# Depthwise convolution with 28 of its 31 taps on TensorE and three on ScalarE and GpSimd

## What is computed

```python
def odd_mixer(h, w_in, dw_w, dw_b, ln_g, ln_b, w_out):
    proj = h @ w_in                                  # 512 x 1024 by 1024 x 3072
    a, b, gate = jnp.split(proj, [CONV_WIDTH, 2 * CONV_WIDTH], axis=-1)
    glu = a * jax.nn.sigmoid(b)
    conv = lax.conv_general_dilated(                 # depthwise, 31 taps, causal
        glu, dw_w.astype(glu.dtype), window_strides=(1,), padding=[(CONV_K - 1, 0)],
        dimension_numbers=('NWC', 'WIO', 'NWC'), feature_group_count=CONV_WIDTH)
    cf = conv.astype(jnp.float32) + dw_b.astype(jnp.float32)
    mu = jnp.mean(cf, axis=-1, keepdims=True)
    var = jnp.mean(jnp.square(cf - mu), axis=-1, keepdims=True)
    cn = (cf - mu) * lax.rsqrt(var + EPS) * ln_g.astype(jnp.float32) + ln_b.astype(jnp.float32)
    y = jax.nn.silu(cn).astype(h.dtype) * jax.nn.silu(gate)
    return y @ w_out
```

## Time and profile before

| | us |
|---|---|
| median of 3 runs | 1090.32 |
| lowest and highest | 1090.15, 1090.68 |
| profiled execution | 1090.47 |
| its span in the trace | 1088.6 |

### The profile page before, as it was taken

How to read it: one execution, slowest core, us unless ns; L and a number is a source line. 1 busy time by engine, 2 the same in 40 slices (tenths; PEclk the granted TensorE clock), 3 DMA queues, 4 the chain that set the end, 5 groups by cost and what they waited for, 6 DMA issues and landing times.

```text
span 1088.6 us, 16129 instructions
## 1 busy us (share of the span) xinstructions
PE 1078.4 (99%) x5872; PEld 873.0 (80%) x5872; DVE 669.1 (61%) x969; ACT 458.9 (42%) x807; POOL 495.0 (45%) x373
## 2 busy tenths in 40 slices
PE   9999999999999999999999999999999999999997
PEld 7788877788888888888888888877778878888786
DVE  6877966327856676667631222558754668886863
ACT  6334421445653333333323333345464643244663
POOL 4444631132645444444444444533348577532541
PEclk9999999999999999999999999999999999999999
DMA  9953621331323232323232324322115222212222
GB/s 247 137 90 62 93 52 29 114 81 39 106 89 114 79 104 88 113 79 105 88 106 71 104 95 140 114 78 79 39 44 149 70 67 78 78 40 79 77 78 77
DMA packets 101721, 97.27 MB, mean 89 GB/s; under 512 B 4896, under 2 KB 95776, under 8 KB 101280
## 3 DMA queue, kind: packets, MB, share of 16 engines
q1 hardware_dynamic: 101232, 95.71, 32.3%
q10 hardware_dynamic: 432, 0.79, 0.2%
HBM read 94.38 MB, written 2.10 MB: 89 GB/s over the span
## 4 chain that ended last, share of the span: by engine, by line
PE 93%; DVE 2%; ACT 1%; POOL 1%; DMA 1%; issue 1%; SPq 0%; POOLq 0%; DVEq 0%; ACTq 0%
PE ps L1985 26%; PE ps L1986 26%; PE ps L1987 26%; PE ps L2559 4%; POOL w_lo L543 1%; PE ps L2223 1%; DVE conv L1829 1%; DMA raw<-in_w_in 1%; PE ps L2493 1%; PE ps L2504 1%; DVE tt L1392 1%; PE ps L2481 1%; PE ps L2273 1%; PE ps L2258 0%; PE ps L2541 0%
## 5 line engine op out<-in xcount | busy, mean ns | idle before, releaser
L543 POOL TENSOR_TENSOR w_lo<-raw,w_hi 128x512 fp32r<-128x512 f32 (+1 forms) x330 | 446.1, 1362 | 564.6 <-ACT w_hi L664 564.2
L664 ACT ACTIVATE w_hi<-raw 128x512 fp32r<-128x512 f32 (+1 forms) x330 | 201.1, 621 | 252.7 <-PE ps L1987 234.4
L1985 PE MATMUL ps<-x_a,w_hi 128*128 128x512 f32 x616 | 248.0, 403 | 1.9 <-POOL w_lo L543 1.8
L1987 PE MATMUL ps<-x_a,w_lo 128*128 128x512 f32 x616 | 240.2, 390 | 0.0
L1986 PE MATMUL ps<-x_a,w_hi 128*128 128x512 f32 x616 | 240.2, 390 | 0.0
L1985 PE MATMUL ps<-x_b,w_hi 128*128 128x512 f32 x416 | 162.5, 391 | 0.0
L1987 PE MATMUL ps<-x_b,w_lo 128*128 128x512 f32 x416 | 161.9, 389 | 0.0
L1986 PE MATMUL ps<-x_b,w_hi 128*128 128x512 f32 x416 | 161.9, 389 | 0.0
L1985 PEld LDWEIGHTS ps<-x_a,w_hi 128*128 128x128 f32 x616 | 115.7, 188 | 34.8 <-issue 8.9
L1986 PEld LDWEIGHTS ps<-x_a,w_hi 128*128 128x128 f32 x616 | 115.8, 188 | 24.5 <-issue 2.2
L1987 PEld LDWEIGHTS ps<-x_a,w_lo 128*128 128x128 f32 x616 | 115.6, 188 | 24.6
(11 more groups left out here) (362 smaller groups left out, 1511.3 us busy)
## 6 DMA issues: line engine op xcount, KB each, us to landing
raw<-in_w_up SPq DMA_DIRECT2D x44, 512.0 KB, 4.3
raw<-in_w_in SPq DMA_DIRECT2D x31, 512.0 KB, 8.1
raw<-in_c_w_in SPq DMA_DIRECT2D x24, 512.0 KB, 4.6
raw<-in_a_w_in SPq DMA_DIRECT2D x18, 512.0 KB, 4.5
raw<-in_w_down SPq DMA_DIRECT2D x16, 512.0 KB, 3.9
raw<-in_w_out SPq DMA_DIRECT2D x8, 512.0 KB, 4.0
raw<-in_c_w_out SPq DMA_DIRECT2D x8, 512.0 KB, 4.5
raw<-in_w_down SPq DMA_DIRECT2D x8, 384.0 KB, 3.4
```

The lines of the kernel that those rows point to most:

```text
L543: nc.gpsimd.tensor_tensor(ring_half(WL, n), raw_half(n), f32(ring_half(WH, n)), SUB) \
L664: nc.scalar.activation(ring_half(WH, n), raw_half(n), ACT.Copy).then_inc(w_hi, 1)
L1985: mm(out, w_hi_, x_hi_, start=first, stop=False)
L1987: return mm(out, w_lo_, x_hi_, start=False, stop=last)
```

## The change

TensorE does 28 taps in seven steps of four phases (`TAP_STEPS` = 7). The rows of padding ahead of `glu_hi` and `glu_lo` fall from 28 to 24, and the tap weights from 1024 to 896 elements for each partition. The three oldest taps are done apart:

- ScalarE (`old_products`) multiplies glu, moved by 30, 29 and 28 tokens, by tap 0, 1 and 2, into three buffers `OLDP`. Their first tokens are zeroed once by GpSimd. In its queue the three stand behind the four copies of the same tile.
- GpSimd (`old_taps`) adds the three buffers into `OLD`, of which there are two; for k >= 3 it also subtracts MEAN. In its queue this stands after the subtractions and tap weights of n = 2k+6.
- VectorE (`add_old`) adds OLD and the bias to `conv` right after the phase additions, and waits for GpSimd's sum there. For k >= 3 this takes the place of `center`. For k < 3 `center` comes later as before, now as a plain subtraction of MEAN. The step of tile 0 into ACC goes.
- TensorE's next convolution, and `ln_sums`, wait for `phases_read`, raised by the last phase addition, and no longer for `cv_ready`.
- `glu(k)` now also waits until the products of tile k-2 have been read out.

```diff
-TAP_STEPS = 8
+TAP_STEPS = 7
+OLD_TAPS = CK - TAP_PHASES * TAP_STEPS
...
+            def old_taps(k):
+                gp.wait_ge(old_made, OLD_TAPS * (k + 1))
+                if k >= 2:
+                    gp.wait_ge(cv_ready if k < 5 else centered, k - 1)
+                d = OLD[:, k % 2, :]
+                done = k + max(0, k - 3)
+                nc.gpsimd.tensor_tensor(d, OLDP[0], OLDP[1], ADD).then_inc(old_step, 1)
+                gp.wait_ge(old_step, done + 1)
+                if k < 3:
+                    nc.gpsimd.tensor_tensor(d, d, OLDP[2], ADD).then_inc(old_ready, 1)
+                    return
+                gp.wait_ge(bank_free, M7 + SHIFT_AFTER + 2)
+                nc.gpsimd.tensor_tensor(d, d, OLDP[2], ADD).then_inc(old_step, 1)
+                gp.wait_ge(old_step, done + 2)
+                nc.gpsimd.tensor_tensor(d, d, MEAN, SUB).then_inc(old_ready, 1)
...
+                if 0 <= u - U7 - 6 < 2 * KT and (u - U7) % 2 == 0:
+                    old_taps((u - U7 - 6) // 2)
...
+            def old_products(k):
+                act.wait_ge(glu_ready, k + 1)
+                act.wait_ge(tap_parts, 12)
+                if k >= 1:
+                    act.wait_ge(old_ready, k)
+                for i in range(OLD_TAPS):
+                    late = CK - 1 - i
+                    nc.scalar.activation(OLDP[i][:, late:S], GLU[:, k % 2, 0:S - late], ACT.Copy,
+                                         scale=DCW[:, i, k:k + 1]).then_inc(old_made, 1)
...
+                if n % 2 == 0 and 0 <= n // 2 - 2 < KT:
+                    old_products(n // 2 - 2)
...
+                    dve.wait_ge(old_made, OLD_TAPS * (k - 1))
...
-                            ins.then_inc(cv_ready, 1)
+                            ins.then_inc(phases_read, 1)
...
+            def add_old(k, done):
+                dve.wait_ge(dchain, steps[0])
+                dve.wait_ge(phases_read, k + 1)
+                dve.wait_ge(old_ready, k + 1)
+                v.scalar_tensor_tensor(out=CV[:, k, :], in0=CV[:, k, :], scalar=vec("dw_b", k),
+                                       in1=OLD[:, k % 2, :], op0=ADD, op1=ADD).then_inc(done, 1)
...
-                v.scalar_tensor_tensor(out=CV[:, k, :], in0=CV[:, k, :], scalar=vec("dw_b", k), in1=MEAN,
-                                       op0=ADD, op1=SUB).then_inc(centered, 1)
+                v.tensor_tensor(CV[:, k, :], CV[:, k, :], MEAN, SUB).then_inc(centered, 1)
...
                     add_phases(k)
-                    if k == 0:
-                        dve.wait_ge(cv_ready, 1)
-                        step(v.tensor_scalar(ACC[:, :], CV[:, 0, :], vec("dw_b", 0), None, ADD))
-                    elif k == 1:
+                    add_old(k, cv_ready if k < 3 else centered)
+                    if k == 1:
...
-                    pe.wait_ge(cv_ready, k)
+                    pe.wait_ge(phases_read, k)
```

More of the change, by code:

```diff
@@ L58 @@
 TAP_PHASES = 4
-TAP_STEPS = 8
+TAP_STEPS = 7
+OLD_TAPS = CK - TAP_PHASES * TAP_STEPS
+DELAY = CK - OLD_TAPS
 HEAD = TAP_PHASES * (TAP_STEPS - 1)
@@ L262, in build @@
         TW = at("tap_w", [P, 4, 2, TAP_STEPS, P], F32R, AR + 16384)
+        OLD = at("old_taps", [P, 2, S], F32, AR + 16384 + 28672)
+        OLDP01 = at("old_tap_products", [P, 2, S], F32, A3 + 37824)
+        OLDP2 = at("old_tap_product2", [P, S], F32, A3 + 54208)
+        OLDP = (OLDP01[:, 0, :], OLDP01[:, 1, :], OLDP2[:, :])
         ABUF = at("a_buf", [P, 4, S], F32, A3 + 41920)
@@ L327, in build @@
         gate_done, head_gated = sem("gate_silu"), sem("head_gated")
+        old_made, old_step, old_ready = sem("old_taps_products"), sem("old_taps_step"), sem("old_taps_summed")
+        phases_read = sem("conv_phases_read")
         res_copied = sem("late_residual_copied")
@@ L588, in tap_parts_made @@
                         .then_inc(tap_parts, 1)
+                for i in range(OLD_TAPS):
+                    nc.gpsimd.memset(OLDP[i][:, 0:CK - 1 - i], 0.0).then_inc(tap_parts, 1)
                 gp.wait_ge(tap_rounded, 1)
@@ L591, in tap_parts_made @@
                     .then_inc(tap_parts, 1)
-                gp.wait_ge(tap_parts, 9)
+                gp.wait_ge(tap_parts, 12)
             def tap_weights(k, parts=(0, 1)):
@@ L605, in tap_weights @@
                     w = TW0[:, part, :, :] if k == 0 else TW[:, k % 4, part, :, :]
+                    first, n = 1 + OLD_TAPS, TAP_PHASES * TAP_STEPS
                     nc.gpsimd.tensor_tensor(w.rearrange("p j (q c) -> p (j q) c", c=32),
-                                            EYE32[:, :].unsqueeze(1).broadcast_to([P, 32, 32]),
-                                            f32(taps[:, :, k]).unsqueeze(2).broadcast_to([P, 32, 32]), MUL) \
+                                            EYE32[:, :].unsqueeze(1).broadcast_to([P, n, 32]),
+                                            f32(taps[:, first:first + n, k]).unsqueeze(2)
+                                            .broadcast_to([P, n, 32]), MUL) \
                         .then_inc(tapw_ready, 1)
@@ L1140, in gated @@
                 act.wait_ge(glu_ready, k + 1)
-                act.wait_ge(tap_parts, 9)
+                act.wait_ge(tap_parts, 12)
                 if k >= 2:
@@ L1811, in glu @@
                 dve.wait_ge(g_hi, k + 1)
-                dve.wait_ge(tap_parts, 9)
+                dve.wait_ge(tap_parts, 12)
                 if k >= 2:
@@ L1834, in add_phases @@
                             steps[0] += 1
+            def add_old(k, done):
[4 more added lines that the diff above has]
+                                       in1=OLD[:, k % 2, :], op0=ADD, op1=ADD).then_inc(done, 1)
             def center(k):
-                dve.wait_ge(dchain, steps[0])
                 dve.wait_ge(cv_ready, k + 1)
-                v.scalar_tensor_tensor(out=CV[:, k, :], in0=CV[:, k, :], scalar=vec("dw_b", k), in1=MEAN,
-                                       op0=ADD, op1=SUB).then_inc(centered, 1)
+                v.tensor_tensor(CV[:, k, :], CV[:, k, :], MEAN, SUB).then_inc(centered, 1)
             def add_centered(k):
@@ L1896, in _ @@
                     add_phases(k)
-                    if k == 0:
-                        dve.wait_ge(cv_ready, 1)
-                        step(v.tensor_scalar(ACC[:, :], CV[:, 0, :], vec("dw_b", 0), None, ADD))
-                    elif k == 1:
+                    add_old(k, cv_ready if k < 3 else centered)
+                    if k == 1:
                         dve.wait_ge(cv_ready, 2)
-                        v.scalar_tensor_tensor(out=ACC[:, :], in0=CV[:, 1, :], scalar=vec("dw_b", 1),
-                                               in1=ACC[:, :], op0=ADD, op1=ADD).then_inc(shift_sum, 1)
+                        v.tensor_tensor(ACC[:, :], CV[:, 0, :], CV[:, 1, :], ADD).then_inc(shift_sum, 1)
                     elif k == 2:
@@ L1912, in _ @@
                         add_centered(2)
-                    else:
-                        center(k)
+                    elif k >= 3:
                         if k == 3:
@@ L2570, in ln_sums @@
             def ln_sums():
-                pe.wait_ge(cv_ready, KT)
+                pe.wait_ge(phases_read, KT)
                 pe.wait_ge(dsum_ready, 1)
```

## The result

The changed kernel takes 1104.25 us (median of four runs, 1104.0 to 1105.37) against 1090.46 us for the kernel before, measured beside it: 1.0128 times as long (95% interval 1.0116 to 1.0141). That is slower by 13.8 us. The forecast was 1103.0, with a range of 1089 to 1107.

What follows compares the result with a forecast made beforehand. TensorE was taken to set the time, VectorE a close second. The new loop through VectorE, ScalarE and GpSimd loses 9.3 us by the last convolution and 3.4 in the tail, 12.7 on 1090.47: 1103 us (1089 to 1107).

Steps and rivals of the forecast that it cites:

- Which loop becomes the bound: Convolution stage: the loop through VectorE, ScalarE and GpSimd becomes the bound, at 17.6 us against today's 16.87.
- The plain loop: From one tile's rounding of glu to the next: 11.15 us to GpSimd's sum, then 4.3 and 2.17, together 17.6.
- The late sum: VectorE's add_old waits for GpSimd's sum: 3.0 us in tile 0, 2 in tile 1, about 0.5 in a plain tile.
- The turns: VectorE operations with two SBUF inputs alternate with GpSimd's subtractions: add_old and two additions take 4.3 us instead of 1.95.
- rival two: In the convolution stage GpSimd and VectorE hardly meet beyond today's collisions: 1088 us, or 1086; chance 0.15.
- Rival three: Only half the alternations between VectorE and GpSimd happen, 7.6 us less: 1095 us (1089 to 1098); chance 0.17.
- T(7) and the tail: Last tile's convolution matmuls end at 1014.3 instead of 1005.04; the stretch to TensorE's sum over DSUM grows by 3.4 us.
- Rival four: Longer pauses of TensorE in the convolution stage also lower its granted clock: above 1107 us; chance 0.06.
- main case: VectorE and GpSimd alternate fully in the convolution stage: 1103 us; chance 0.62.

Runs made afterwards that it cites:

- the eighth step: The changed kernel with an eighth convolution step per tile put back on TensorE (step 6 done twice): 1105.3 us, ratio 1.0136.
- The held subtractions: The changed kernel, with GpSimd in tiles 3 to 7 waiting after its sum until VectorE has evicted the unit behind its additions: 1096.08 us, ratio 1.0051.
- the run with the clock kept up: The changed kernel with four more 128x512 matmuls just ahead of TensorE's sums behind the last tile: 1102.77 us, ratio 1.0113.
- the last version: Against the kernel with products and sums both earlier: in tiles 3 and 4 GpSimd's second subtraction stands behind the first addition: 1087.37 us, ratio 0.9973.

## Why the prediction was right, point by point

**Which loop becomes the bound: right.** The starts G(k) of ScalarE's rounding of glu, in us:

| | G(1) | G(2) | G(3) | G(4) | G(5) | G(6) |
|---|---|---|---|---|---|---|
| forecast | 903.0 | 922.2 | 943.5 | 962.8 | 981.0 | 998.6 |
| measured | 902.91 | 921.91 | 943.27 | 962.35 | 980.68 | 998.23 |

```profile
980.68 0.63 ACT L1175 ACTIVATE glu_hi<-glu 128x512 fp32r<-128x512 f32 x1 [0.82 <-DVE glu L1853]
```

The plain loop from here to G(6) is 17.55 us, forecast 17.6, before 15.7. Its parts are 11.23 us to the sum (forecast 11.15), 4.12 for the three operations (4.3) and 2.20 to the next rounding (2.17), so the close agreement owes a little to errors of opposite sign. That TensorE's saving would be lost in it is what the eighth step shows (1.05 us instead of 5.6).

**The late sum: right in place, a little small in size.** Forecast 3.0, 2 and 0.5 us; measured 3.27, 2.14 and 0.77 in tile 3. The three products take 1.8 us (copies end at 1001.71, the rounding starts at 1003.52), not 1.6: products start 0.6 apart, where the passes of the earlier trace rows start 0.54 apart. The third GpSimd operation starts 1.37 us after the one before, so the additions take 4.0 us against a forecast of 4.05.

**The turns: right.** Forecast 4.3 us for the three operations, 4.1 measured in tile 6, and one turn in the tail. The forecast's own terms (2 x 1.25 + 3 x 0.65) add up to 4.45 and not 4.3, so the loop by them would be 17.75 us; the measured size is nearer to the rounded figure. The mean of `add_old` was forecast near 1.9 us, which was too long: it is 1.60, the median 1.66. The forecast rested on the earlier trace rows, from other places in the program. The held subtractions show what the turns alone are worth, 7.2 us with the waits nearly unchanged. They also settle rival two: its premise was that these operations hardly meet. Where they are kept from meeting, `add_old` is at 0.75. Rival three, with half the turns, fails too: VectorE loses 2.1 us in tile 6 (4.1 against 1.95), nearly the whole 2.35 that the forecast had.

**T(7) and the tail: right.** The last convolution matmul ends at 1014.09 (1013.67 + 0.42), forecast 1014.3, and the tail is 14.6 us long instead of 11.4, 3.2 more where 3.4 was forecast. Line 2621 starts at 1028.71, forecast 1029.1.

**The clock: the one term that was left out.** Rival four named it, gave it no size, and put it above 1107 with 6 in 100. The clock did fall, behind the longest pause (3.51 us of waiting). It costs 1.5 us between the medians, and so belongs to the main case instead of a rival. With it the sum closes: 12.3 us to line 2621 and 1.5 of clock are the 13.8 between the medians. The 12.3 us come from one pair of traces, but the run with the clock kept up gives the same between medians (1102.77 against 1090.42). The forecast of 1103 was 1.25 low: the clock was missing (1.5), the 12.7 us to line 2621 were 0.4 too many, and the kernel before was 0.14 us slower in this comparison than the median that the forecast started from. So two errors partly cancel here.

**In the experiments** two estimates failed. The 1094 for the kernel without the wait let too many of the turns end where `add_old` ran earlier, while they went on with the two additions behind it, and it did not name the clock. The 1085.5 for the last version missed the turns that came with the later sum. For the kernel with the filled pause 2.4 us were expected back, and 1.5 came.

## What to carry to other kernels

Moving work off the engine that bounds a stage is worth at most the distance to the next loop, so sum the loop through the helper engines with every handover before counting the saving. An operation on GpSimd beside short VectorE operations with two SBUF inputs costs VectorE most of the GpSimd operation's length (0.9 to 1.1 us of 1.27 here). Look at what stands behind the operation that releases VectorE, and move the helpers' work a tile ahead (here 17 us between two orders of the same work) before judging the idea by its time.

## What the runs showed of the hardware

- VectorE pays for the turns with or without a wait ahead of them. `add_old` on 128x512 floats takes 0.75 us alone and mostly 1.67 (1.32 at the least) beside a GpSimd subtraction of 1.27. An addition takes 0.69 alone and 1.78 beside one, both in the changed kernel and in the run without the wait. GpSimd pays less: two subtractions take 3.00 us together in the turns of tile 6, and 2.50 at 1031.03 in the same trace.
- TensorE's clock was at the lower level (0.50) after the pause ahead of line 2621 (3.51 us of waiting), and at the upper (1.00) all through when four matmuls stood in that pause. In the run with the held subtractions, where TensorE waits 1.39 us ahead of the same line, that matmul pair takes 1.10 us, its length at the upper level. In the run with the eighth step TensorE waits 2.86 us there and the pair takes 2.04 us; without `add_old`'s wait for GpSimd it is 4.31 us of waiting and 2.05.
